# Two decoder layers on one core: the second mixer's end worked head by head, with the output rows in another order

## The chip, the cores and the metric

The kernel runs on one core of a Trainium2 chip. The metric is the device time of one execution, in microseconds. The kernel before took 1078.41 us, the median of three runs (1078.24 to 1080.96). One further execution was profiled; all rows below come from that one.

## The reference

The reference is one inference step through two decoder layers, for 256 prompt tokens and 64 sample tokens (8 sequences of 8), 320 columns in all, 1024 channels. Each layer is a mixer and a mixture of experts. The change lies in the second layer's mixer, whose core is:

```python
def odd_mixer(h, ...):
    gy, xb, q, k, v = split(h @ w_in)                 # 512 channels each
    xc = conv_b + sum(xe[:, i:i + L] * conv_w[i])     # causal, width 4
    r, ig = sigmoid(xc @ rgate_w + rgate_b), sigmoid(xc @ igate_w + igate_b)   # 8 blocks of 64
    log_a = -LRU_C * r * softplus(-lru_lambda);  a = exp(log_a)
    b = sqrt(-expm1(2 * log_a)) * ig * xc             # 1.0 in place of the root at position 0
    b[:, 0] += a[:, 0] * h0
    hs = scan over time of  h = a * h + b
    yc = gelu(gy) * hs
    o = dilated_attn(q, k, v)                         # 8 heads of 64, prompt and sample
    return concatenate([yc, o]) @ w_out
x = x + odd_mixer(rmsnorm(x));  x = x + hier_moe(rmsnorm(x))
```

The last state of the scan is an output too.

## The kernel before

Channels lie on the 128 partitions and tokens along the free axis. A tensor of 512 channels is thus four blocks of 128 x 320. The code calls each block j = 0 to 3; this document calls it a head of the recurrent part where the title does. The work of each engine is written out by hand in one fixed order, with semaphores that count what each engine has done. `MIX1_TENSOR`, `MIX1_SCALAR` and `MIX1_VECTOR` (L85 to L104) name those counts; `tensor_did`, `scalar_did` and `vector_did` wait for one of them. `next_reads` lets an instruction raise a count and makes DVE wait for it, so that its next instruction may read the result.

A weight matrix is used in two parts: `w_hi`, a rounded copy made by ACT, and `w_lo`, the rest, made by DVE. The same is done to the moving operand. A product is then three matmuls for each 128 channels (hi x hi, hi x lo, lo x hi). Weights come in chunks of 1 MB from a stream: SP loads chunk c into a `raw` buffer (`load_chunk`), ACT splits it (`split_hi`, L329), DVE makes the low part (`split_lo`, L341), and a `raw` buffer may be loaded again once `w_lo_made` says that its low part is done. A `w` buffer may be written again once TensorE's `tile_done` says that the rows of its last chunk are through.

The second mixer's output product is 8 rows of 128 channels, two per chunk (`AT_OUT1` to `AT_OUT1 + 3`); row i accumulates in PSUM bank i. `out1_rows` (L3061) makes row i over the channel blocks `ks`: blocks 4 to 7 are the attention's result, held in `attn_hi` and `attn_lo`, blocks 0 to 3 are the recurrent part's, held in `h_hi` and `h_lo`. There are only two `w` buffers in this stage, so the third chunk's split waits for rows 0 and 1, the fourth's for rows 2 and 3.

The stretch that changes is the mixer's end, behind the projection's tile 18:

- TensorE (`mix1_pe`, from L3036): the gates' products 4 to 7 (`gate`, L2871, banks 0 and 1 in turn) among the last attention work; projection tile 19, in bank 1; then, when tile 19 has been read and the attention's low parts are made (`y_lo` at 3), rows 0 to 3 over blocks 4 to 7; when the recurrent part's low parts are made (`y_lo` at 4), rows 0 to 3 over blocks 0 to 3; rows 4 to 7 whole, each followed by a piece of the router's work (`front_pe`).
- ACT (`mix1_act`, from L2535): the gates' tanh (`gate_out`), the square root `lru_root` over all four blocks (L2543), the attention's high parts (L2545 and L2547), half a weight chunk (L2549), gelu over all four blocks (L2551), the recurrent part's high part (L2553).
- DVE (`mix1_dve`, from L2819): `lru_square`; the copies of the last attention results; `lru_in` (L2706); the attention's low parts (L2831); tile 19 out of its bank (`tile_out(19)`); half a weight chunk's low part (L2835); `lru_scan` (L2717: four products with the root's result, called the weighing below; the samples' start values, L2724 to L2726; four scans; two copies of the last states); the product with gelu (L2838); the low part (L2841). Then `out_proj_dve` adds each finished row to `xt`.
- POOL stores the last states when `lru_kept` is counted (L3204). ACT waits for that store, in `moe_act` (L580), before it splits the first chunk of the experts' weights.

Of the kernel before, what the change touches and what calls it, by code (L numbers as in the profile page):

```python
# [16 lines left out]
ALU = mybir.AluOpType  # L17
# [10 lines left out]
HT = 4  # L28
# [49 lines left out]
def counted(*names):  # L78
# [13 lines left out]
                      "s_out2", "gate4", "s_turned30", "s_turned31", "s_turned32", "gate5", "p_turned7", "p_out6", "gate6", "s_values3", "gate7",  # L92
# [59 lines left out]
def decoder_layers(nc, ins, outs, stop=None):  # L152
    with ExitStack() as ctx:
# [2268 lines left out]
        def mix1_act(eng):  # L2422
# [120 lines left out]
            eng.activation(lru_m, lru_m, ACT.Sqrt, scale=0.25).then_inc(S("mix1_scalar"), 1)  # L2543
            vector_did(eng, "p_kept3")
# [4 lines left out]
            out_half(1).then_inc(S("w_hi_made"), 1)  # L2549
            eng.wait_ge(S("in1_taken"), IN1_TILES)  # L2550
            eng.activation(gy, gy, ACT.Gelu_apprx_tanh).then_inc(S("mix1_scalar"), 1)  # L2551
            vector_did(eng, "yc_made")
            eng.activation(h_hi[:, 0:4, :], gy, ACT.Copy).then_inc(S("y_hi"), 1)  # L2553

        def mix1_dve(eng):
# [161 lines left out]
            def lru_scan():  # L2717
                scalar_did(eng, "lru_root")
                next_reads(eng, eng.memset(lru_m[:, :, 0:1], 0.5))
                for j in range(HT):  # L2720
                    last = eng.tensor_tensor(lru_m[:, j, :], lru_m[:, j, :], lru_i[j], ALU.mult)
                next_reads(eng, last)
                starts = lambda v: v[:, :, TP:T].rearrange("p j (b s) -> p j b s", b=NB)[:, :, :, 0]
# [3 lines left out]
                for j in range(HT):  # L2727
                    last = eng.tensor_tensor_scan(lru_t[:, j, :], lru_a[:, j, :], lru_m[:, j, :], 0.0, ALU.mult, ALU.add)
                next_reads(eng, last)
# [93 lines left out]
            lru_square()  # L2823
            sample_masked(3)
            prompt_kept(3)
            sample_kept(3)
            lru_in()
            for n, cols in enumerate((slice(0, TP), slice(TP, T))):
                vector_did(eng, "attn_out3")
                eng.wait_ge(S("y_hi"), n + 2)  # L2830
                eng.tensor_tensor(attn_lo[:, :, cols], q1[:, :, cols], attn_hi[:, :, cols], ALU.subtract).then_inc(S("y_lo"), 1)  # L2831

            tile_out(19)
            eng.wait_ge(S("w_hi_made"), AT_OUT1 + 2)
            out_half_lo(1).then_inc(S("w_lo_made"), 1)  # L2835
            lru_scan()
            scalar_did(eng, "gelu")
# [15 lines left out]
        def mix1_pe(eng, begun):  # L2853
# [198 lines left out]
            for i in range(HT):  # L3052
                out1_rows(eng, i, (4, 5, 6, 7), True, False)
# [337 lines left out]
```

## Time and profile before

| | |
|---|---|
| median of three runs | 1078.41 us (1078.24 to 1080.96) |
| profiled execution | 1070.39 us, its span 1068.5 us |
| TensorE (PE) busy | 1033.6 us, 97% of the span |
| VectorE (DVE) busy | 815.6 us, 76% |
| ScalarE (ACT) busy | 639.8 us, 60% |
| mean granted TensorE clock | 0.989 |
| data moved | 271.04 MB, 254 GB/s over the span |

The span is the time from the first to the last instruction. A busy engine is not an engine at its peak. A matmul's duration includes its way through the array, so that neighbours overlap; what counts is the distance from start to start. The granted clock is given in parts of full speed. Where a line waits for several things, the profile names the one that came last.

### The profile page before, as it was taken

How to read it: one execution, taken by the hardware profiler on the slowest of the kernel's cores; microseconds unless marked ns; L12 is line 12 of the kernel's file. 1: busy time of each engine (PE TensorE's matmuls, PEld its weight loads, DVE VectorE, ACT ScalarE, POOL GpSimd, SP SyncE). 2: the span in 40 equal slices, each digit the busy share in tenths (PEclk: the TensorE clock that was granted, in tenths of full speed). 3: DMA queues.
4: the chain of work that ended last, by engine and by line, in shares of the span. 5: the costliest groups of instructions: out<-in, count | busy, mean ns of one | idle time of the engine just before them, and what ended most of it. 6: DMA issues, size and time to landing. Idle time of an engine off the chain costs nothing.

```text
span 1068.5 us, 17486 instructions
## 1 busy us (share of the span) xinstructions
PE 1033.6 (97%) x7349; PEld 871.5 (82%) x7349; DVE 815.6 (76%) x926; ACT 639.8 (60%) x660; POOL 19.0 (2%) x23
## 2 busy tenths in 40 slices
PE   9999999899999999999999999989999999999995
PEld 8899889877788888888878877677688888888884
DVE  7649545675788998999986677654878999998983
ACT  6556224524677767677755442445677777767664
POOL 0000000000000000000001300000000000000000
PEclk9999999999999999999999999989999999999998
DMA  9333000226399999999958779617199999999951
GB/s 373 132 115 107 21 4 3 73 80 248 133 343 347 368 362 360 362 362 369 354 221 349 296 281 376 257 41 275 53 353 324 375 351 355 357 365 366 372 212 52
DMA packets 40323, 271.04 MB, mean 254 GB/s; under 512 B 5057, under 2 KB 5521, under 8 KB 9521
## 3 DMA queue, kind: packets, MB, share of 16 engines
q1 hardware_dynamic: 39616, 267.11, 66.5%
q0 software_dynamic: 624, 2.76, 0.7%
q8 instruction: 61, 1.00, 0.4%
q14 instruction: 22, 0.17, 0.0%
HBM read 265.78 MB, written 4.07 MB: 253 GB/s over the span
## 4 chain that ended last, share of the span: by engine, by line
PE 84%; DVE 9%; ACT 3%; DMA 2%; issue 1%; ACTq 0%; SPq 0%; DVEq 0%
PE ps L925 11%; PE ps L927 11%; PE ps L926 11%; PE ps L959 5%; PE ps L961 5%; PE ps L960 5%; PE ps L352 3%; PE ps L354 3%; PE ps L353 3%; PE ps L1855 3%; DVE w_lo L346 2%; DMA raw<-in_stream 1%; PE ps L971 1%; PE ps L938 1%; PE ps L972 1%
## 5 line engine op out<-in xcount | busy, mean ns | idle before, releaser
L346 DVE TENSOR_TENSOR w_lo<-raw,w_hi 128x2048 fp32r<-128x2048 f32 x74 | 171.2, 2315 | 32.8 <-ACT w_hi L336 32.6
L336 ACT ACTIVATE w_hi<-raw 128x2048 fp32r<-128x2048 f32 x74 | 141.6, 1914 | 64.4 <-PE ps L927 25.8
L346 DVE TENSOR_TENSOR lo_more<-raw_more,hi_more 128x2048 fp32r<-128x2048 f32 x48 | 109.9, 2289 | 17.9 <-ACT hi_more L336 17.9
L346 DVE TENSOR_TENSOR lo_more<-raw,hi_more 128x2048 fp32r<-128x2048 f32 x48 | 109.9, 2290 | 11.9 <-ACT hi_more L336 11.9
L346 DVE TENSOR_TENSOR w_lo<-raw_more,w_hi 128x2048 fp32r<-128x2048 f32 x47 | 107.6, 2290 | 14.6 <-ACT w_hi L336 14.5
L336 ACT ACTIVATE hi_more<-raw 128x2048 fp32r<-128x2048 f32 x48 | 91.9, 1916 | 25.6 <-PE ps L927 25.6
L336 ACT ACTIVATE w_hi<-raw_more 128x2048 fp32r<-128x2048 f32 x47 | 90.1, 1917 | 16.2 <-PE ps L961 16.2
L336 ACT ACTIVATE hi_more<-raw_more 128x2048 fp32r<-128x2048 f32 x48 | 91.9, 1915 | 11.0 <-PE ps L961 9.6
L352 PE MATMUL ps<-h_hi,w_hi 128*128 128x320 f32 x272 | 87.1, 320 | 1.1 <-DVE arena L2579 1.1
L354 PE MATMUL ps<-h_hi,w_lo 128*128 128x320 f32 x272 | 84.6, 311 | 0.0
L353 PE MATMUL ps<-h_lo,w_hi 128*128 128x320 f32 x272 | 84.6, 311 | 0.0
L925 PE MATMUL ps<-hi_more,h_hi 128*128 128x512 f32 x170 | 68.1, 401 | 0.0
L926 PE MATMUL ps<-lo_more,h_hi 128*128 128x512 f32 x170 | 66.4, 391 | 0.0
L927 PE MATMUL ps<-hi_more,h_lo 128*128 128x512 f32 x170 | 66.3, 390 | 0.0
L925 PE MATMUL ps<-w_hi,h_hi 128*128 128x512 f32 x150 | 60.1, 401 | 0.0
L926 PE MATMUL ps<-w_lo,h_hi 128*128 128x512 f32 x150 | 58.5, 390 | 0.0
L927 PE MATMUL ps<-w_hi,h_lo 128*128 128x512 f32 x150 | 58.5, 390 | 0.0
L352 PEld LDWEIGHTS ps<-h_hi,w_hi 128*128 128x128 f32 x272 | 51.6, 190 | 5.0 <-issue 3.8
L959 PE MATMUL ps<-w_hi,hid_hi 128*128 128x512 f32 x136 | 53.5, 393 | 0.0
L961 PE MATMUL ps<-w_hi,hid_lo 128*128 128x512 f32 x136 | 53.0, 389 | 0.0
L960 PE MATMUL ps<-w_lo,hid_hi 128*128 128x512 f32 x136 | 52.9, 389 | 0.0
L353 PEld LDWEIGHTS ps<-h_lo,w_hi 128*128 128x128 f32 x272 | 51.8, 190 | 0.2
(538 smaller groups left out, 2401.8 us busy)
## 6 DMA issues: line engine op xcount, KB each, us to landing
raw<-in_stream SPq DMA_DIRECT2D x125, 1024.0 KB, 6.8
raw_more<-in_stream SPq DMA_DIRECT2D x96, 1024.0 KB, 6.9
arena<-in_k_near SPq DMA_DIRECT2D x6, 1024.0 KB, 10.4
arena<-in_v_near SPq DMA_DIRECT2D x5, 1024.0 KB, 7.6
arena<-in_k_far SPq DMA_DIRECT2D x6, 512.0 KB, 8.7
kv_spare<-in_v_near SPq DMA_DIRECT2D x3, 1024.0 KB, 8.8
arena<-in_v_far SPq DMA_DIRECT2D x5, 512.0 KB, 6.8
kv_spare<-in_k_near SPq DMA_DIRECT2D x2, 1024.0 KB, 13.5
```

The costliest lines, as they stand in the source:

```text
L336: eng.activation(hi_slot(W_SLOT[c]), raw_chunk(c), ACT.Copy).then_inc(S("w_hi_made"), 1)
L346: eng.tensor_tensor(lo_slot(W_SLOT[c]), raw_chunk(c), hi_slot(W_SLOT[c]), ALU.subtract).then_inc(S("w_lo_made"), 1)
L352: eng.matmul(ps[:, bank, 0:T], hi[:, m, k, :], x_hi[:, k, :], start=(k == 0), stop=False)
L353: eng.matmul(ps[:, bank, 0:T], hi[:, m, k, :], x_lo[:, k, :], start=False, stop=False)
L354: mm = eng.matmul(ps[:, bank, 0:T], lo[:, m, k, :], x_hi[:, k, :], start=False, stop=(k == KT - 1))
L925: eng.matmul(out, xh, hi[:, k, :], start=(n == 0 and k == 0), stop=False)
L926: eng.matmul(out, xh, lo[:, k, :], start=False, stop=False)
L927: mm = eng.matmul(out, xl, hi[:, k, :], start=False, stop=(n == 1 and k == 3))
L959: eng.matmul(out, hh[:, k, :], hi[:, k, :], start=(e % 4 == 0 and k == 0), stop=False)
L960: eng.matmul(out, hh[:, k, :], lo[:, k, :], start=False, stop=False)
L961: mm = eng.matmul(out, hl[:, k, :], hi[:, k, :], start=False, stop=(e % 4 == 3 and k == HT - 1))
L1855: mm = eng.matmul(at_head(bank, s, o), lhs[o:o + 64, s, :], rhs[o:o + 64, s, :], start=True, stop=True)
```

## The change

The last gate's product moves ahead of the last sample values on TensorE. ACT takes gelu of three blocks right behind the square root, ahead of the attention's high parts, and the fourth block's gelu and the recurrent part's high parts block by block behind them. `lru_starts` and `lru_kept` hold the instructions of the old scan's L2723 to L2726 and L2730 to L2731. On DVE the weighing is taken apart and moved ahead of the attention's low parts; tile 19 leaves its bank behind the first scan; scan, product with gelu and low part go block by block, and the half weight chunk and the last states come behind them. TensorE makes rows 0 and 2, then 1, over the attention's blocks; row 0 follows the recurrent blocks one by one; row 3's attention half comes behind row 1.

```diff
@@ tables @@
-                      "s_out2", "gate4", "s_turned30", "s_turned31", "s_turned32", "gate5", "p_turned7", "p_out6", "gate6", "s_values3", "gate7",
+                      "s_out2", "gate4", "s_turned30", "s_turned31", "s_turned32", "gate5", "p_turned7", "p_out6", "gate6", "gate7", "s_values3",
-                      "out_hi", "s_tok30", "s_tok31", "s_tok32", "p_tok7", "lru_root", "gelu")
+                      "out_hi", "s_tok30", "s_tok31", "s_tok32", "p_tok7", "lru_root", "gelu_most", "gelu")
-                      "s_masked3", "p_kept3", "attn_out3", "lru_kept", "yc_made")
+                      "s_masked3", "p_kept3", "attn_out3", "yc0", "yc1", "yc2", "yc3", "lru_kept")
@@ mix1_act @@
             eng.activation(lru_m, lru_m, ACT.Sqrt, scale=0.25).then_inc(S("mix1_scalar"), 1)
+            eng.wait_ge(S("in1_taken"), IN1_TILES - 1)
+            eng.activation(gy[:, 0:3, :], gy[:, 0:3, :], ACT.Gelu_apprx_tanh).then_inc(S("mix1_scalar"), 1)
             vector_did(eng, "p_kept3")
             eng.activation(attn_hi[:, :, 0:TP], q1[:, :, 0:TP], ACT.Copy).then_inc(S("y_hi"), 1)
             vector_did(eng, "attn_out3")
             eng.activation(attn_hi[:, :, TP:T], q1[:, :, TP:T], ACT.Copy).then_inc(S("y_hi"), 1)
-            out_half(1).then_inc(S("w_hi_made"), 1)
             eng.wait_ge(S("in1_taken"), IN1_TILES)
-            eng.activation(gy, gy, ACT.Gelu_apprx_tanh).then_inc(S("mix1_scalar"), 1)
-            vector_did(eng, "yc_made")
-            eng.activation(h_hi[:, 0:4, :], gy, ACT.Copy).then_inc(S("y_hi"), 1)
+            eng.activation(gy[:, 3, :], gy[:, 3, :], ACT.Gelu_apprx_tanh).then_inc(S("mix1_scalar"), 1)
+            for j in range(HT):
+                vector_did(eng, f"yc{j}")
+                eng.activation(h_hi[:, j, :], gy[:, j, :], ACT.Copy).then_inc(S("y_hi"), 1)
+                if j == 1:
+                    out_half(1).then_inc(S("w_hi_made"), 1)
@@ mix1_dve: lru_scan is taken apart into @@
+            def lru_weigh(js):
+                scalar_did(eng, "lru_root")
+                if js[0] == 0:
+                    next_reads(eng, eng.memset(lru_m[:, :, 0:1], 0.5))
+                for j in js:
+                    last = eng.tensor_tensor(lru_m[:, j, :], lru_m[:, j, :], lru_i[j], ALU.mult)
+                next_reads(eng, last)
+            def lru_starts():
...
+            def lru_scan(j):
+                next_reads(eng, eng.tensor_tensor_scan(lru_t[:, j, :], lru_a[:, j, :], lru_m[:, j, :], 0.0, ALU.mult, ALU.add))
+            def yc(j):
+                scalar_did(eng, "gelu" if j == 3 else "gelu_most")
+                eng.tensor_tensor(gy[:, j, :], gy[:, j, :], lru_t[:, j, :], ALU.mult).then_inc(S("mix1_vector"), 1)
+            def yc_lo(j):
+                vector_did(eng, f"yc{j}")
+                eng.wait_ge(S("y_hi"), j + 4)
+                eng.tensor_tensor(h_lo[:, j, :], gy[:, j, :], h_hi[:, j, :], ALU.subtract).then_inc(S("y_lo"), 1)
+            def lru_kept():
...
@@ mix1_dve, its end @@
             lru_square()
+            lru_in()
             sample_masked(3)
+            lru_weigh((0, 1))
             prompt_kept(3)
+            lru_weigh((2,))
             sample_kept(3)
-            lru_in()
+            lru_weigh((3,))
             for n, cols in enumerate((slice(0, TP), slice(TP, T))):
...
                 eng.tensor_tensor(attn_lo[:, :, cols], q1[:, :, cols], attn_hi[:, :, cols], ALU.subtract).then_inc(S("y_lo"), 1)
+            lru_starts()
+            lru_scan(0)
             tile_out(19)
+            yc(0)
+            lru_scan(1)
+            yc(1)
+            yc_lo(0)
+            lru_scan(2)
+            yc(2)
+            yc_lo(1)
+            lru_scan(3)
+            yc(3)
+            yc_lo(2)
+            yc_lo(3)
             eng.wait_ge(S("w_hi_made"), AT_OUT1 + 2)
             out_half_lo(1).then_inc(S("w_lo_made"), 1)
-            lru_scan()
-            scalar_did(eng, "gelu")
-            eng.tensor_tensor(gy, gy, lru_t, ALU.mult).then_inc(S("mix1_vector"), 1)
-            vector_did(eng, "yc_made")
-            eng.wait_ge(S("y_hi"), 4)
-            eng.tensor_tensor(h_lo[:, 0:4, :], gy, h_hi[:, 0:4, :], ALU.subtract).then_inc(S("y_lo"), 1)
+            lru_kept()
@@ mix1_pe @@
             gate(6)
+            gate(7)
             sample_values(3)
-            gate(7)
             prompt_values(7)
             sample_out(3)
             in1_tile(19)
+            eng.wait_ge(S("gate_taken"), 2 * HT)
+            eng.wait_ge(S("y_lo"), 3)
+            out1_rows(eng, 0, (4, 5, 6, 7), True, False)
+            out1_rows(eng, 2, (4, 5, 6, 7), True, False)
             eng.wait_ge(S("in1_taken"), IN1_TILES)
-            eng.wait_ge(S("y_lo"), 3)
+            out1_rows(eng, 1, (4, 5, 6, 7), True, False)
             for i in range(HT):
-                out1_rows(eng, i, (4, 5, 6, 7), True, False)
-            eng.wait_ge(S("y_lo"), 4)
-            for i in range(HT):
-                out1_rows(eng, i, (0, 1, 2, 3), False, True).then_inc(S("tile_done"), 1)
+                if i == 2:
+                    out1_rows(eng, 3, (4, 5, 6, 7), True, False)
+                out1_rows(eng, i, (0, 1, 2, 3), False, True, i == 0).then_inc(S("tile_done"), 1)
@@ out1_rows @@
+                if follow:
+                    eng.wait_ge(S("y_lo"), 4 + k)
```

## Rows read from the trace of the kernel before

**Rows 1.** The page, part 4: the chain that ended last, shares of the span

```profile
PE 84%; DVE 9%; ACT 3%; DMA 2%; issue 1%; ACTq 0%; SPq 0%; DVEq 0%
```

**Rows 2.** Windows: each engine's busy us (x instructions), TensorE clock, DMA share, GB/s

```profile
122.00:124.00 2.00, 0.50 (x20) 0.29 (x13) 1.93 (x4) 0.00 (x0) 0.00 (x0) 1.00 0.00 0
...
193.00:199.00 6.00, 6.00 (x64) 5.38 (x63) 4.25 (x4) 1.26 (x3) 0.00 (x0) 0.72 0.02 5
...
707.90:710.40 2.50, 0.03 (x1) 0.00 (x0) 1.45 (x2) 1.02 (x1) 0.54 (x1) 1.00 0.03 7
...
712.30:717.10 4.80, 4.80 (x18) 4.80 (x19) 0.49 (x1) 0.00 (x0) 0.00 (x0) 0.50 0.01 3
...
765.00:1050.00 285.00, 284.99 (x1330) 236.24 (x1329) 247.65 (x158) 203.53 (x144) 0.00 (x0) 1.00 0.87 326
```

**Rows 3.** TensorE's waits, 685 to 760 us: total us, times, longest

```profile
PE ps L3072 <- DVE h_lo L2841: 4.4, 1, 4.4
PE ps L971 <- DVE select_r L742: 1.1, 1, 1.1
PE ps L3072 <- DVE w_lo L346: 0.9, 1, 0.9
PE ps L3072 <- DVE arena L2579: 0.8, 1, 0.8
```

**Rows 4.** Timeline of TensorE: start us, us, line, output and inputs, x count

```profile
689.66 0.81 PE L2874 MATMUL ps<-arena 128*128 128x320 f32 x2
...
705.13 0.31 PE L3072 MATMUL ps<-attn_hi,w_hi 128*128 128x320 f32 x1
...
706.01 0.31 PE L3072 MATMUL ps<-attn_hi,w_hi 128*128 128x320 f32 x1
```

**Rows 5.** The chain in order of time, 670 to 780 us: start us, us, what

```profile
699.87 1.07 ACT w_hi L2477
...
712.30 0.63 PE ps L3072
...
718.40 1.92 ACT w_hi L336
...
722.70 0.41 PE ps L3072
```

**Rows 6.** Timeline of ACT; in brackets its idle time before, and what ended it

```profile
694.95 1.28 ACT L2543 ACT_TABLE_LOAD   x1
...
700.94 1.28 ACT L2551 ACT_TABLE_LOAD   x1
702.24 1.28 ACT L2551 ACTIVATE arena<-arena 128x1280 f32<-128x1280 f32 x1
```

**Rows 7.** Timeline of DVE, 690 to 713 us

```profile
690.68 1.49 DVE L2715 SCALAR_TENSOR_TENSOR arena<-arena 128x1280 f32<-128x1280 f32 x1
...
696.34 1.29 DVE L2709 SCALAR_TENSOR_TENSOR attn_low<-attn_low,arena 128x320 f32<-128x320 f32 x3
...
698.59 1.56 DVE L2831 TENSOR_TENSOR attn_lo<-arena,attn_hi 128x1024 fp32r<-128x1024 f32 x2 [0.57 <-ACT attn_hi L2545]
700.07 0.48 DVE L2579 TENSOR_TENSOR arena<-ps,arena 128x320 f32<-128x320 f32 x1
...
702.24 1.30 DVE L2721 TENSOR_TENSOR arena<-arena,attn_low 128x320 f32<-128x320 f32 x3
...
703.98 0.22 DVE L2724 TENSOR_TENSOR arena<-arena 128x32 f32<-128x32 f32 x1
...
704.68 2.97 DVE L2728 TENSOR_TENSOR_SCAN arena<-arena 128x320 f32<-128x320 f32 x4
...
710.75 1.49 DVE L2841 TENSOR_TENSOR h_lo<-arena,h_hi 128x1280 fp32r<-128x1280 f32 x1 [1.40 <-ACT h_hi L2553]
```

**Rows 8.** DMA issues, 700 to 765 us: queue, count, KB each, median us to landing

```profile
raw<-in_stream SPq DMA_DIRECT2D x5, 1024.0 KB, 4.9
...
out_lru<-state POOLq DMA_DIRECT2D x1, 18.0 KB, 1.7
```

More of the change, by code:

```diff
@@ L2715, in lru_square @@
                 eng.scalar_tensor_tensor(flat(lru_m), flat(lru_t), 1.0, flat(lru_m), ALU.add, ALU.mult).then_inc(S("mix1_vector"), 1)
-            def lru_scan():
+            def lru_weigh(js):
                 scalar_did(eng, "lru_root")
-                next_reads(eng, eng.memset(lru_m[:, :, 0:1], 0.5))
-                for j in range(HT):
+                if js[0] == 0:
+                    next_reads(eng, eng.memset(lru_m[:, :, 0:1], 0.5))
+                for j in js:
                     last = eng.tensor_tensor(lru_m[:, j, :], lru_m[:, j, :], lru_i[j], ALU.mult)
                 next_reads(eng, last)
+            def lru_starts():
                 starts = lambda v: v[:, :, TP:T].rearrange("p j (b s) -> p j b s", b=NB)[:, :, :, 0]
@@ L2726, in lru_scan @@
                 next_reads(eng, eng.memset(starts(lru_a), 0.0))
-                for j in range(HT):
-                    last = eng.tensor_tensor_scan(lru_t[:, j, :], lru_a[:, j, :], lru_m[:, j, :], 0.0, ALU.mult, ALU.add)
-                next_reads(eng, last)
+            def lru_scan(j):
[8 more added lines that the diff above has]
+            def lru_kept():
                 eng.tensor_copy(lru_out[:, :, 0:1], lru_t[:, :, TP - 1:TP])
@@ L3059, in mix1_pe, with out1_rows @@
                 front_pe(eng, 1, i)
-        def out1_rows(eng, i, ks, start, stop):
+        def out1_rows(eng, i, ks, start, stop, follow=False):
             c = AT_OUT1 + i // 2
```

## The prediction

> **What bounds the kernel now.** I read the chain first: 84% of it is TensorE [rows 1]. So a microsecond counts only where TensorE waits or runs slowly. The windows say where that is not: from 765 to 1050 us TensorE is busy 284.99 of 285 us at full clock [rows 2], so the expert stage cannot shrink, only start earlier. TensorE's own waits between 685 and 760 us say where it is: the longest, 4.4 us, is for `h_lo` of L2841, and another 0.9 us is for the weights' low part [rows 3]. Behind the 4.4 us comes a second cost. In 707.90 to 710.40 TensorE is all but idle at full clock; the 18 matmuls of 712.30 to 717.10 run at a granted 0.50, which is 1.2 GHz [rows 2]. They take 4.80 / 18 = 0.267 us each. At 1.00, 2.4 GHz, six of the same matmuls take 0.88 us (705.13 to 706.01), 0.147 each [rows 4]. The slow stretch costs 18 x 0.120 = 2.2 us.
>
> The end of the stretch is the chain: output rows 0 and 1 need all of `h_lo` (712.30), then ACT splits the third weight chunk (718.40), DVE makes its low part, and row 4 starts at 722.70 [rows 5]. I take the start of row 4 as the mark; everything behind it hangs on it.
>
> **Part 1, the last gate's product first.** A gate's product lasts 0.81 us, about 0.73 from start to start [rows 4]. gate(7) moves ahead of the sample values of pair 3, which move back by as much; TensorE's sum stays. It now follows gate(6), which began at 689.66, and ends near 691.2, so its tanh leaves ACT near 691.8. ACT's square root waited for that tanh alone: its table load started at 694.95, right behind it [rows 6], while the other input, `lru_square`, was done at 690.68 + 1.49 = 692.17 [rows 7]. So root: 692.2 + 1.28 + 1.28 = 694.8. The sample output waits for a masked product that comes 0.7 us later; the last prompt values, which TensorE runs in between at their old time, cover it. Cost 0 (0 to +0.2).
>
> **Part 2, gelu of three heads ahead of the attention's split.** It adds one table load of 1.28 and 960 columns. 1280 columns took 1.28 [rows 6], so about 1.0. ACT: 694.8 + 2.3 = 697.1, when the attention split may begin; its first 1024 columns take 1.05 (estimate, from 1280 in 1.28). That is sooner than `attn_lo` had them, at 698.59 [rows 7], so nothing is lost. On DVE `lru_in` (three in 1.29 [rows 7] and a fourth of 0.48, to about 694.0), the masked product, three weighings and the two copies lie ahead of it, and end near 697.7. The four weighings (1.29 + 0.48 = 1.8, from 702.24 on [rows 7]) come off the tail. DVE then waits for ACT's first `attn_hi` near 698.15, and `attn_lo`, 1.56 for two [rows 7], ends near 699.7. Tile 19's last result is there before 699.87, when ACT, waiting for it, starts [rows 5]. TensorE thus begins rows 0 and 2 at 699.75; before, it began 0.8 us later, waiting for DVE to empty tile 19's bank (L2579) [rows 3]. That wait goes, since these two rows use other banks.
>
> The row on the table load shows the switch whole: ACT's work of 699.87 ran 1.07 us [rows 5], the load began at 700.94, gelu at 702.24 [rows 6]. The Trainium skill, "ScalarE: Activation LUTs", section "What ACT_TABLE_LOAD costs", gives a load of about 1283 ns and a drain of about 1380 ns on top. The load agrees with the trace, the drain does not show. By that rule the two switches ahead of the attention split would cost 2.8 us more and the time would be about 1073.8; this case's row 700.94 speaks against it. What such a mechanism would do here, in this trace's own numbers, is rival B.
>
> **Part 3, DVE's tail by heads.** Pitches from the rows [rows 7]: a 320-column product lasts 0.48, and three in 1.29 give a pitch of 0.41. Four scans took 2.97 without a wait between; one scan with its round trip is 0.83 (estimate: 0.80 and 0.03). The sample starts take 704.68 - 703.98 = 0.70. From `attn_lo`'s end at 699.7:
> starts 0.70, scan 0 0.83, tile 19 out 0.41, yc0 0.41: 702.05. Scan 1 0.83, yc1 0.41, low 0 0.41: 703.7. Scan 2, yc2, low 1, again 1.65: 705.35. Scan 3 0.83, yc3 0.41, low 2 0.41: 707.0. Low 3 waits for ACT's copy of head 3 (yc3 ends at 706.66; the copy, a quarter of 1280 columns plus start, about 0.46), begins at 707.2 and ends at 707.7.
> Before, `h_lo` ended at 710.75 + 1.49 = 712.24 [rows 7]. The 4.5 us are: weighings 1.8, the second half of the weight split with the wait ahead of it 1.6 (now last), the ACT hand-over of 1.4 (now beside the next head), less the finer grain. Tile 19 leaves its bank 1.2 us later, at 701.7. Row 1 wants it at 703.3, behind 24 matmuls of rows 0 and 2, so that wait is covered; without the new order it would show. ACT's copies fit: head 0 at 702.3 behind the last gelu, head 1 at 703.4, then half a weight chunk of 1.07 [rows 5] to 704.9, head 2 at 705.05 (low 2 wants it at 706.6).
>
> **Part 4, output rows in another order.** 36 matmuls at 0.147 are 5.3 us: 699.75 to 705.05. Then row 0 follows the heads: k0 to 705.5 (its low part is there at 703.8), k1 to 706.0, k2 waits until 707.1, k3 until 707.75. Idle 1.1 + 0.2 us against 4.4. Row 0 is issued by 708.2, row 1 by 710.0. Its last matmul lasts 0.31 [rows 4]: ACT begins the third chunk at 710.2, and the old 4.3 us (718.40 to 722.70 [rows 5]) give 714.5. TensorE meanwhile has row 3's attention half and both last halves, 36 matmuls, to 715.25. The weights are no longer late; row 4 starts at 715.25. The low part of the second half chunk (1024 columns, about 1.2 against 1.49 for 1280 [rows 7], now 707.65 to 708.9) is wanted at 710.0.
>
> **What is moved later.** That low part frees a buffer for the first expert chunk: SP issues its load at 708.9 instead of near 702.2, where the old low part ended (the weighings follow it at 702.24 [rows 7]), and it lands after a median 4.9 us [rows 8], near 714. ACT wants it near 719, behind the fourth chunk and a table load. The LRU rows are stored from about 709.7, a little over 1 us later than before, with 1.7 us to landing [rows 8], against ACT's wait for them near 719. Both cost 0, with 5 us to spare.
>
> **The sum.** 722.70 - 715.25 = 7.45 us. The same from the terms: `h_lo` 4.5 earlier; behind it 15 matmuls of 2.2 in place of 24 with the slow clock, 5.9: 3.7; together 8.2; less 0.8 of the old wait for weights that is now work: 7.4. Behind row 4 all waits keep their distances (ACT's token squares come 1 us closer, but their readers had 2 us and more), and the expert stage is TensorE without a gap. I take 7.4 us. The profiled execution took 1070.39 us (span 1068.5), 8.0 under the median of 1078.41. The stretch is fixed work, so I subtract the same: **1078.4 - 7.4 = 1071.0 us**. Bounds of the doubtful terms: the scan's round trip between 0.74 (a quarter of 2.97) and 0.9 moves the sum by +0.3 to -0.3; starts and copies by 0.3; the clock below.
>
> **Rivals.**
> A. The clock falls all the same. TensorE still has 1.3 us of idle near 706 to 707.8. For a fall: in 193 to 199 us the clock stood at a mean of 0.72 although TensorE was busy throughout [rows 2], so a dense row of matmuls does not exclude it. Against: in 122 to 124 us TensorE was busy only 0.50 of 2 us and stayed at 1.00, and in 707.90 to 710.40 it held through 2.5 us [rows 2]; here dense work surrounds a shorter gap. Price as before, 2.2 us: 1073.2. Chance 0.10.
> B. A table switch with work queued behind it costs a second time its 1.28 us [rows 6], because ACT empties first. There are two ahead of the attention split, 2.6 us. The split, `attn_lo` and DVE's tail are all 2.6 later, TensorE starts at 702.3, and row 4 at 717.85. Gain 4.85: 1073.6. Against it is the gapless row 700.94. Chance 0.03.
> C. No visible change: the gain returns as a later wait behind row 4, for instance DVE's additions and the tokens' low parts, ahead of which the same FIFO now has the LRU rows. It needs more than 4.2 us of new waiting, while TensorE's only longer wait there besides those counted is one of 1.1 us [rows 3]. About 1077. Chance 0.08.
> D. Slower: the first expert chunk's load, issued 6.7 us later. ACT stands at its split with all token work behind it. Tokens' squares and copies take 5 us behind the load, the low parts 1.9, and TensorE wants them near 731. So a landing up to 724 is free; from 724 + 7.4 = 731.4 on, 22.5 us after issue, the kernel is slower, one for one. For it: ACT is strictly in order. Against: median 4.9 us [rows 8] and an almost empty queue. At 25 us: 1081. Chance 0.04.
> The forecast has 0.75, its own range 1070.2 to 1072.2. Runs of before spread over 2.7 us, so 0.3% (3.2 us) is what can be told from no change. Range 1069.5 to 1075.8: below, the bounds' 0.6 and 0.9 for the runs' spread; above, A and B together (1071.0 + 2.2 + 2.6). Faster 0.87 (forecast, A, B, less a margin), same 0.08, slower 0.05.
>
> **What would show it.** Right: TensorE's wait for `h_lo` about 1.3 us in place of 4.4; granted clock 1.00 from 700 to 725; row 4 starting 15.5 us after the first attention matmul of the output (before 22.1) with no wait for weights; one gelu load near 694.8; `tile 19` out about 1.6 us behind `attn_lo`. Wrong: a clock of 0.50 behind 707; a gap between the square root and gelu; TensorE waiting for tile 19's bank ahead of row 1; ACT waiting on the first expert chunk's DMA; or a saving at row 4 that is gone at 765.

## The result and the profile after

The changed kernel took a median of 1066.92 us in 12 runs. The kernel before took 1075.14 us in 12 runs (1069.88 to 1080.96), among them the three that the forecast started from. One run of the changed kernel (1280.74 us at a mean granted clock of 0.747) and one of `rows_paired` below (1709.39 us at 0.552) were disturbed: without them the two medians are 1066.61 us (1062.63 to 1072.61) and 1064.70 us, and every ratio leaves them out. The ratio is 0.9936, with a 95% interval of 0.9914 to 0.9958: 6.9 us faster, and the interval excludes no change. A second series (`after_again`, below) gave 1067.51 against 1072.84, ratio 0.9939 (0.9913 to 0.9964), or 6.5 us. The medians by themselves lie 8.2 and 5.3 us apart in the two series; I go by the ratios. The forecast was 1071.0 us with a range of 1069.5 to 1075.8, or a ratio of 1071.0 / 1078.41 = 0.9931. So size and mechanism came out, and the absolute time fell below the range. Both halves of that need showing.

The two profiled executions mislead by their totals: 1070.39 us before (span 1068.5), 1070.92 us after (span 1069.1). I therefore measure from a place that both have: the start of DVE's second `lru_square` pass. It is at 690.68 us before [rows 7] and at 699.16 after. Nothing that leads up to it was changed; only gate(7), moved forward on TensorE, begins some 0.3 us ahead of it. In the table every time is counted from that place, which I call the mark. "Row 4" is the start of output row 4, "router" the start of DVE's first instruction of the router, L719 (`router_filled`'s expectation calls it the weighing, which is not the recurrent part's weighing), and "end" the span's end, known to 0.1 us.

```
                        before                  after
first row, attention    9.93                    8.73
row 4                  32.02                   24.12
router (L719)          57.30                   49.32
end                   377.82                  369.94
```

The changed kernel gains 7.90 us at row 4 and still 7.88 at the end, while its execution was 0.5 us longer. The missing 8.5 us (699.16 - 690.68) lie ahead of the mark, in code that is the same; `before_second` below shows that they come from the first mixer. The kernel before was profiled twice more there, with row 4 at 32.43 and 32.30, so the gain at row 4 is 7.9 to 8.3 us. TensorE's waits in the changed kernel, 685 to 760 us (in total, times, longest), against [rows 3]:

```profile
PE ps L971 <- DVE select_r L742: 1.1, 1, 1.1
PE ps L3106 <- DVE h_lo L2745: 0.8, 1, 0.8
PE ps L524 <- DVE hot L730: 0.4, 1, 0.4
```

The wait of 4.4 us for `h_lo` is now 0.8; those for tile 19's bank (0.8) and for the weights' low part (0.9) are gone. Here are its windows from the mark to the first row, to the start of row 0's last block, to row 4, and over the stretch that the prediction named, in the columns of [rows 2]:

```profile
699.16:707.89 8.73, 8.73 (x96) 6.86 (x95) 7.92 (x18) 6.99 (x8) 0.00 (x0) 1.00 0.07 26
707.89:715.70 7.81, 7.02 (x47) 6.51 (x46) 7.33 (x16) 3.24 (x6) 0.00 (x0) 1.00 0.00 0
715.70:723.28 7.58, 7.58 (x52) 7.58 (x52) 4.82 (x7) 1.92 (x1) 0.55 (x1) 1.00 0.40 143
...
700.00:725.00 25.00, 24.21 (x198) 22.25 (x189) 19.71 (x40) 12.77 (x15) 0.55 (x1) 1.00 0.18 58
```

The granted clock is 1.00 throughout, where the 18 matmuls behind the old gap ran at 0.50 [rows 2]. TensorE's rows of the timeline: the first attention product, the only listed wait, row 4.

```profile
707.89 0.31 PE L3106 MATMUL ps<-attn_hi,w_hi 128*128 128x320 f32 x1
...
715.00 0.41 PE L3106 MATMUL ps<-h_hi,w_hi 128*128 128x320 f32 x1 [0.79 <-DVE h_lo L2745]
...
723.28 0.31 PE L3106 MATMUL ps<-h_hi,w_hi 128*128 128x320 f32 x1
```

From the first to the last are 15.39 us (before 22.09; forecast 15.5). ACT, against [rows 6], shows the one thing better than forecast:

```profile
699.53 0.53 ACT L2439 ACTIVATE arena<-ps,half_bias 128x320 f32<-128x320 f32 x1
700.08 1.28 ACT L2543 ACT_TABLE_LOAD   x1
701.37 1.27 ACT L2543 ACTIVATE arena<-arena 128x1280 f32<-128x1280 f32 x1
702.66 1.28 ACT L2545 ACT_TABLE_LOAD   x1
703.96 1.00 ACT L2545 ACTIVATE arena<-arena 128x960 f32<-128x960 f32 x1
704.87 1.04 ACT L2547 ACTIVATE attn_hi<-arena 128x1024 fp32r<-128x1024 f32 x1
```

The square root's table load starts at 700.08, right behind the last tanh, while its input `lru_square` ends only at 700.65 (the first row of DVE's fence below: 699.16 + 1.49). The forecast had put the load behind that input. The first profile of the kernel before already had loads that ran ahead of a late input, and also one that did not:

```profile
593.94 1.28 ACT L2483 ACT_TABLE_LOAD   x1
599.09 0.20 ACT L2483 ACTIVATE state<-state 128x4 f32<-128x4 f32 x1 [3.86 <-DVE state L2598]
...
608.86 1.28 ACT L2461 ACT_TABLE_LOAD   x1 [5.88 <-DVE state L2641]
```

What decides between the two no run here shows. DVE of the changed kernel, against [rows 7]:

```profile
699.16 1.49 DVE L2719 SCALAR_TENSOR_TENSOR arena<-arena 128x1280 f32<-128x1280 f32 x1
...
706.04 1.56 DVE L2852 TENSOR_TENSOR attn_lo<-arena,attn_hi 128x1024 fp32r<-128x1024 f32 x2 [0.29 <-ACT attn_hi L2547]
...
708.22 0.82 DVE L2736 TENSOR_TENSOR_SCAN arena<-arena 128x320 f32<-128x320 f32 x1
709.07 0.49 DVE L2583 TENSOR_TENSOR arena<-ps,arena 128x320 f32<-128x320 f32 x1
709.48 0.48 DVE L2740 TENSOR_TENSOR arena<-arena 128x320 f32<-128x320 f32 x1
...
715.15 0.49 DVE L2745 TENSOR_TENSOR h_lo<-arena,h_hi 128x320 fp32r<-128x320 f32 x1 [0.20 <-ACT h_hi L2555]
```

The last low part ends at 715.64, 16.48 from the mark; before, 21.56. Of that 5.08, 4.54 is what part 3 of the prediction had. The other 0.54 fits the earlier table load (0.57): ACT goes from it to `attn_hi` without a gap, and DVE waits 0.29 us for `attn_hi` in the row of 706.04. No run moved the load alone.

### The profile page after: what moved, and what is told of

It is laid out like the page before. It is cut to its first block, busy times and chain, and to the rows that moved or that the text cites. A ratio compares the mean times of both kernels' runs of the same rounds, so it can differ in the third digit from the quotient of the medians.

```text
span 1069.1 us, 17507 instructions
## 1 busy us (share of the span) xinstructions
PE 1038.7 (97%) x7349; PEld 876.2 (82%) x7349; DVE 816.1 (76%) x932; ACT 640.6 (60%) x664; POOL 18.8 (2%) x23
## 4 chain that ended last, share of the span: by engine, by line
PE 85%; DVE 8%; ACT 3%; DMA 2%; issue 1%; SPq 1%; ACTq 0%; DVEq 0%
PE ps L925 11%; PE ps L927 11%; PE ps L926 11%; PE ps L959 5%; PE ps L961 5%; PE ps L960 5%; PE ps L352 3%; PE ps L353 3%; PE ps L354 3%; PE ps L1855 3%; DMA raw<-in_stream 2%; PE ps L971 1%; PE ps L938 1%; DVE w_lo L346 1%; PE ps L972 1%
```

## Experiments

Four questions: what is each part worth, how much of it is clock, where does the run-to-run level come from, and where do the timed 6.5 to 6.9 us lose a little against 7.9. The four undoings come first; each is the changed kernel with one part taken back, seen in one profile. The number that counts is row 4's start, 24.12 in the changed kernel.

**gate_back.**

```diff
@@ mix1_pe, and the same in MIX1_TENSOR @@
             gate(6)
-            gate(7)
             sample_values(3)
+            gate(7)
```

> The changed kernel with one part undone: gate(7) again behind the sample values of pair 3. The measure is the distance from the start of DVE's second lru_square pass (which lies ahead of everything that was changed) to TensorE's start of output row 4: 32.0 us in the kernel before, 24.1 in the changed one. Theory: everything on ACT and DVE hangs on the last gate's tanh now, because lru_in stands ahead of the sample's masked product. The tanh ends near 703.4 on the changed kernel's scale instead of 700.06, so root, gelu and the attention's split come 3.3 us later and the distance is 27.2 +- 0.4. Rival: as my forecast had it, the gate's place is a matter of order on TensorE whose cost is covered; then 24.1 to 24.4.

Measured: 27.45 from the mark, 3.3 us later than in the changed kernel; 1069.8 us. TensorE's longest waits, and DVE's rows that they hang on:

```profile
PE ps L2993 <- DVE arena L2652: 2.3, 1, 2.3
PE ps L3106 <- DVE h_lo L2745: 0.9, 1, 0.9
```

```profile
697.60 1.30 DVE L2713 SCALAR_TENSOR_TENSOR attn_low<-attn_low,arena 128x320 f32<-128x320 f32 x3 [2.79 <-ACT arena L2439]
...
699.53 0.48 DVE L2652 SCALAR_TENSOR_TENSOR arena<-ps,state,consts 128x256 f32<-128x256 f32 x1
```

DVE's queue now has `lru_in` ahead of the sample's masked product; with the gate late, `lru_in` waits 2.79 us for its tanh, the masked product behind it is late, and TensorE's sample output waits 2.3 us for that. So the gate's place is worth 3.3 us here, because it lets `lru_in` and the recurrent part's weighing stand so early. What it would gain alone, in the kernel before, was not run.

**gelu_behind.**

```diff
             eng.activation(lru_m, lru_m, ACT.Sqrt, scale=0.25).then_inc(S("mix1_scalar"), 1)
-            eng.wait_ge(S("in1_taken"), IN1_TILES - 1)
-            eng.activation(gy[:, 0:3, :], gy[:, 0:3, :], ACT.Gelu_apprx_tanh).then_inc(S("mix1_scalar"), 1)
...
             eng.activation(attn_hi[:, :, TP:T], q1[:, :, TP:T], ACT.Copy).then_inc(S("y_hi"), 1)
+            eng.activation(gy[:, 0:3, :], gy[:, 0:3, :], ACT.Gelu_apprx_tanh).then_inc(S("mix1_scalar"), 1)
```

> The changed kernel with the gelu of the first three blocks put behind the attention's high parts. Distance as above (24.1 in the changed kernel). Theory: ACT stands idle for 3.4 us behind the attention's high parts, which holds the table load of 1.28 and the 1.0 of gelu, and ahead of them it waits for DVE's copy of the attention's result anyway; so 24.1, between 24.0 and 24.3. Rival: the early gelu is what lets the heads follow each other, and behind it the first product with gelu waits for the table: 25.1 to 26.4.

Measured: 24.00, 0.1 us earlier than with gelu ahead; 1068.17 us. ACT in this kernel:

```profile
700.85 1.06 ACT L2545 ACTIVATE attn_hi<-arena 128x1024 fp32r<-128x1024 f32 x1 [2.09 <-DVE arena L2680]
701.82 0.40 ACT L2547 ACTIVATE attn_hi<-arena 128x256 fp32r<-128x256 f32 x1
702.23 1.28 ACT L2549 ACT_TABLE_LOAD   x1
703.53 1.01 ACT L2549 ACTIVATE arena<-arena 128x960 f32<-128x960 f32 x1
```

Gelu moved behind the split ends at 704.54 and still has over 1 us of idle behind it; ahead of the split it fills the 2.1 us that ACT here waits for DVE. Both places are free, so gelu's place ahead of the split is worth nothing. This does not price part 2 as a whole: the old place, all four blocks behind tile 19's reading, was not run. By this kernel's rows it would be late: ACT begins the fourth block at 709.60 in the changed kernel, and a load of 1.28 and 1280 columns in 1.28 [rows 6] from there end near 712.2, where the first product with gelu now begins at 709.48 (an estimate).

**rows_old.** TensorE makes the output rows in the old order.

```diff
-            eng.wait_ge(S("gate_taken"), 2 * HT)
-            eng.wait_ge(S("y_lo"), 3)
-            out1_rows(eng, 0, (4, 5, 6, 7), True, False)
-            out1_rows(eng, 2, (4, 5, 6, 7), True, False)
             eng.wait_ge(S("in1_taken"), IN1_TILES)
-            out1_rows(eng, 1, (4, 5, 6, 7), True, False)
+            eng.wait_ge(S("y_lo"), 3)
+            for i in range(HT):
+                out1_rows(eng, i, (4, 5, 6, 7), True, False)
+            eng.wait_ge(S("y_lo"), 7)
             for i in range(HT):
-                if i == 2:
-                    out1_rows(eng, 3, (4, 5, 6, 7), True, False)
-                out1_rows(eng, i, (0, 1, 2, 3), False, True, i == 0).then_inc(S("tile_done"), 1)
+                out1_rows(eng, i, (0, 1, 2, 3), False, True).then_inc(S("tile_done"), 1)
```

> The changed kernel with TensorE's old order: rows 0 to 3 over the attention's blocks behind tile 19's reading, then a wait for all four recurrent low parts, then rows 0 to 3. Theory: the start waits for tile 19's bank (709.6 instead of 707.9), 48 matmuls end at 716.7, behind the last low part, rows 0 and 1 end near 720.2 and the third chunk's two splits of 4.35 us are late again by 1.2 us: 25.7 +- 0.3. Rival: only the 1.1 us of idle within row 0 moves elsewhere and the order is worth nothing: 24.1 +- 0.3.

Measured: 27.59, 3.5 us later; 1075.93 us. TensorE's waits from the mark to the router's start:

```profile
PE ps L3103 <- DVE w_lo L2771: 1.7, 1, 1.7
PE ps L3103 <- DVE arena L2583: 1.6, 1, 1.6
PE ps L3103 <- DVE w_lo L346: 0.9, 1, 0.9
```

The wait for tile 19's bank (L2583) is the one the prediction said the new order covers. That for the half chunk's low part (L2771) I had not counted in the expectation, which was 1.9 us too low: in the changed DVE order that low part comes last, and the old row order wants it for row 3's attention half, ahead of all recurrent blocks. Row order and DVE order only work together.

**heads_off.** The new orders stay, but scan, gelu product, `h_hi` and `h_lo` are each done over four blocks again, as before.

```diff
@@ mix1_act @@
-            for j in range(HT):
-                vector_did(eng, f"yc{j}")
-                eng.activation(h_hi[:, j, :], gy[:, j, :], ACT.Copy).then_inc(S("y_hi"), 1)
-                if j == 1:
-                    out_half(1).then_inc(S("w_hi_made"), 1)
+            out_half(1).then_inc(S("w_hi_made"), 1)
+            vector_did(eng, "yc3")
+            eng.activation(h_hi[:, 0:4, :], gy, ACT.Copy).then_inc(S("y_hi"), 4)
@@ mix1_dve: four scans, tile_out(19) behind the first, then @@
+            eng.tensor_tensor(gy, gy, lru_t, ALU.mult).then_inc(S("mix1_vector"), 4)
+            vector_did(eng, "yc3")
+            eng.wait_ge(S("y_hi"), 7)
+            eng.tensor_tensor(h_lo[:, 0:4, :], gy, h_hi[:, 0:4, :], ALU.subtract).then_inc(S("y_lo"), 4)
```

> The changed kernel with scans, product with gelu, high and low part in whole passes again (the weighing stays ahead, the last weights stay behind, the rows keep their new order). Theory: the last low part comes only 0.35 us later (716.0), but row 0 can't begin before it; rows 0 and 1 end 1.7 us later and row 4 starts at 24.85 + 0.8 = 25.7 +- 0.3. TensorE then idles near 2.9 us ahead of row 0; the clock may fall, which adds up to 2.2 (27.9). Rival: the split by heads is the main part of the gain (my forecast named the hand-over of 1.4 and the overlap): 27 or more with the clock at full.

Measured: 25.99, 1.9 us later; 1071.23 us, with one wait:

```profile
PE ps L3100 <- DVE h_lo L2861: 3.0, 1, 3.0
```

TensorE stood still for 3.0 us and the clock stayed at 1.00 behind it; in the kernel before it fell behind 4.4. The blocks are worth 1.9 us (the whole passes on ACT and DVE together), about half of what one might read out of 4.4 against 0.8.

The undoings sum to 3.3 - 0.1 + 3.5 + 1.9 = 8.6 us against a gain of 7.9: the parts lean on each other. Each rests on one profile. Now the other side, the kernel before with one thing added.

**gap_filled.** 28 matmuls that do nothing fill the wait for `h_lo`.

```diff
@@ the kernel before, mix1_pe, ahead of the recurrent half of the rows @@
+            for _ in range(28):
+                eng.matmul(ps[:, 5, 0:T], attn_hi[:, 0, 0:P], attn_hi[:, 0, :], start=True, stop=True)
             eng.wait_ge(S("y_lo"), 4)
```

> The kernel before with 28 dummy matmuls of 320 columns (their result is never read) put into TensorE's idle time ahead of the wait for the recurrent low parts. Distance from DVE's second lru_square pass to row 4: 32.0 in the kernel before. Theory: the clock of 0.50 behind the gap is owed to the gap; filled, it stays at 1.00, rows 0 and 1 take 3.5 instead of 5.7 us, and the distance is 29.8 +- 0.2. Rival: the fall comes from something else, or the dummies push row 0 back: 32.0 or more.

Measured: row 4 at 29.81 from the mark, against 32.02: 2.2 us, which is the prediction's 18 x 0.120. Against the two later profiles of the kernel before (32.43 and 32.30) it is 2.6 and 2.5. The wait for `h_lo` is down to 0.3. Its clock where the 18 matmuls run now:

```profile
722.00:724.00 2.00, 2.00 (x16) 2.00 (x15) 0.49 (x1) 0.00 (x0) 0.00 (x0) 1.00 0.00 0
```

The execution as a whole took 1078.41 us, above the 1072.90 of the kernel before timed beside it. The mark lies at 699.55 us here, against 690.68 in the first profile: it is again the stretch ahead of the mark that is long.

**weigh_alone.** The kernel before with the recurrent part's weighing right behind `lru_in`.

```diff
             lru_in()
+            lru_weigh()
@@ and lru_scan() without these four products @@
```

> The kernel before with one part done alone: the four weighing products ahead of the attention's low parts. Theory: 1.8 us leave the tail, but 1.3 of them push the attention's low parts, tile 19's reading and the weight half back, since ACT's high parts are there first, less 0.4 us of a wait that goes: the last low part comes 0.9 us earlier and the distance is 31.1 +- 0.3 if the clock still falls, 28.9 if it does not. Rival: the whole 1.8 us are gained, 30.2.

Measured: 28.72, 3.3 us earlier than before, though the clock did fall. TensorE's waits for DVE, and windows around the fall:

```profile
PE ps L3075 <- DVE arena L2579: 2.2, 1, 2.2
...
PE ps L3075 <- DVE h_lo L2844: 0.5, 1, 0.5
```

```profile
706.00:707.00 1.00, 0.63 (x4) 0.64 (x5) 1.00 (x2) 0.99 (x2) 0.00 (x0) 1.00 0.00 0
707.00:711.00 4.00, 4.00 (x19) 4.00 (x18) 3.83 (x8) 0.94 (x1) 0.00 (x0) 0.57 0.66 209
711.00:713.00 2.00, 2.00 (x16) 2.00 (x15) 1.68 (x4) 0.26 (x1) 0.54 (x1) 1.00 0.30 116
...
717.00:724.00 7.00, 6.13 (x42) 5.87 (x41) 3.49 (x4) 2.85 (x2) 0.00 (x0) 1.00 0.00 0
```

I had expected 31.1 with a fall and 28.9 without. The fall moved: it now follows the earlier wait of 2.2 us and slows the attention half of the rows, which had idle time behind it to lose (the wait for `h_lo` is 0.5 in place of 4.4). The slow clock thus cost nothing at row 4, and 2.2 us of clock and 1.06 of an earlier `h_lo` (20.50 against 21.56 from the mark) make the 3.3. So the weighing alone is worth only 1.06 on DVE's tail, not 1.8. That the fall moved because of the longer first wait (2.2 in place of 0.8) is read from one profile and not tested.

**after_again** and **rows_paired**, timed together. The first is the changed kernel once more. In the second, output rows 0 and 1 alternate between the blocks as these come, which gives TensorE work for its last wait.

```diff
-            for i in range(HT):
-                if i == 2:
-                    out1_rows(eng, 3, (4, 5, 6, 7), True, False)
-                out1_rows(eng, i, (0, 1, 2, 3), False, True, i == 0).then_inc(S("tile_done"), 1)
+            for k in range(HT):
+                eng.wait_ge(S("y_lo"), 4 + k)
+                for i in range(2):
+                    mm = out1_rows(eng, i, (k,), False, k == HT - 1)
+                    if k == HT - 1:
+                        mm.then_inc(S("tile_done"), 1)
+            out1_rows(eng, 3, (4, 5, 6, 7), True, False)
+            for i in range(2, HT):
+                out1_rows(eng, i, (0, 1, 2, 3), False, True).then_inc(S("tile_done"), 1)
```

> The changed kernel once more, beside the kernel before on the same chip. Theory: the absolute time of a run is set by how long the clock stands at half in the first mixer, which the change does not touch, so the medians of both kernels move together by several us between sessions while their difference stays: ratio 0.992 to 0.995 (6 to 8 us). The distance to row 4 is 24.1. Rival: the profiled pair, 1068.5 before and 1069.1 after, shows that the gain is lost elsewhere: ratio 0.998 to 1.000.

> The changed kernel with rows 0 and 1 following the recurrent blocks together (block 0 for both rows, block 1 for both, and so on). Theory: six matmuls instead of three stand ahead of each wait, which covers the 0.8 and 0.3 us that TensorE still idles; row 4 starts 1.1 us earlier, distance 23.0 +- 0.2, time 1.1 us below the changed kernel (0.1%, at the edge of what the timing shows). Rival: the third chunk's split, which waits for both rows, or the low part of the second half chunk becomes the bound and the distance stays at 24.1.

Measured: `after_again` 24.11 from the mark, so in the changed kernel the stretch repeats to 0.01 us. `rows_paired` 23.05, with no wait of TensorE left between the mark and the router's start. Timed, the ratio is 0.994 (0.991 to 0.9969) against 0.9939: the 1.1 us are in the profile and can't be told in the runs, which spread over 8 us. (The median of all 8 runs is 1067.08 us, of 7 of them 1064.70.)

**thin_mixed.** `rows_paired` with 12 wide matmuls that do nothing among the thin ones of the first mixer, where the clock falls near 67 us.

```diff
+            def wide():
+                for _ in range(2):
+                    eng.matmul(ps[:, 6, 0:T], h_hi[:, 0, 0:P], h_hi[:, 0, :], start=True, stop=True)
@@ behind each of the sums over a head, L1650 and L1697 @@
+                    wide()
```

> As rows_paired, and in the first mixer 12 dummy matmuls of 320 columns (never read) are mixed into the 48 matmuls of one or two columns ahead of which the clock fell near 66 to 69 us in both profiles. Theory: that fall is owed to a stretch of thin matmuls, not to idle time; the dummies cost 1.8 us and save the fall there, 2 to 5 us: the profile has no clock below 1.00 between 60 and 80 us and the time is 0 to 3 us below rows_paired. Rival: the fall comes anyway or moves, and the time is 1.8 us above rows_paired.

Measured: the clock falls all the same, for 11 us; 1069.66 us (12 runs, ratio 0.995, 0.9926 to 0.9973). The theory failed; the rival, the cost of the added work on top of `rows_paired`, is what remains.

```profile
66.00:67.00 1.00, 1.00 (x11) 1.00 (x10) 0.36 (x3) 1.00 (x1) 0.00 (x0) 1.00 0.00 0
67.00:78.00 11.00, 11.00 (x50) 11.00 (x49) 2.54 (x3) 0.31 (x1) 0.00 (x0) 0.53 0.29 95
```

TensorE was busy in every microsecond around it. Thin matmuls at that place are not the cause, or 12 wide ones are not enough; which, I did not try.

**before_second** and **before_third**, the kernel before profiled twice more.

> The kernel before, unchanged, profiled a second time, to see whether what the change removed is there in every execution. If it is: from the start of the second lru_square pass, output row 4 begins 32.0 us later, with a stretch of half clock of nearly 7 us behind the wait for the gelu product's low part, as in the first profile, and the change is worth 7.9 us in every execution. If the clock falls there only in some executions: 29.8 us, and the change is worth 5.7 us in these, which would put the timed 6.5 to 6.9 us between the two. The span itself is to differ from the first profile's 1068.5 us by up to 10 us, by half clock in the first mixer.

> As the second profile of the kernel before: 32.0 us from the second lru_square pass to output row 4 if the clock falls in the gap each time, 29.8 us where it does not.

Measured: row 4 at 32.43 and 32.30 from the mark (32.02 in the first profile), each time behind a wait of 4.4 us and with the clock down. The second took 1080.88 us, the third 1071.33. Windows of 60 to 80 and 193 to 213 us, first of the kernel before in the first profile, then of its second one, then of the changed kernel's profile:

```profile
60.00:80.00 20.00, 20.00 (x153) 19.34 (x153) 7.31 (x17) 12.28 (x23) 0.00 (x0) 0.91 0.30 106
193.00:213.00 20.00, 18.50 (x172) 16.51 (x170) 11.89 (x10) 10.58 (x14) 0.00 (x0) 0.89 0.24 77
```

```profile
60.00:80.00 20.00, 20.00 (x117) 20.00 (x117) 6.82 (x13) 10.34 (x20) 0.00 (x0) 0.74 0.30 105
193.00:213.00 20.00, 18.02 (x186) 15.66 (x183) 8.99 (x10) 12.61 (x15) 0.54 (x1) 0.57 0.18 60
```

```profile
60.00:80.00 20.00, 20.00 (x117) 20.00 (x117) 6.42 (x14) 9.63 (x19) 0.00 (x0) 0.74 0.31 105
193.00:213.00 20.00, 18.02 (x163) 15.39 (x158) 8.99 (x10) 12.95 (x15) 0.54 (x1) 0.57 0.17 60
```

The last two agree, and the first does not: the same code gets a mean clock of 0.57 or 0.89 in 193 to 213 us, whichever kernel it belongs to. Over all 16 profiles the mark lies at 690.7 us where the two windows have the highest clocks (`before`: 0.91 and 0.89; `rows_paired`: 0.91 and 0.91), and near 699 us or later wherever they are at 0.74 to 0.83 and 0.57 to 0.60, except for 697.43 in `router_filled_second`. Why the clock is low for longer in one execution than in another no run shows. The mark lies at 690.68, 700.80 and 699.16 us in these three; 10.1 of the 10.5 us between the two profiles of before (1080.88 - 1070.39) are there. The timed runs fit: over 21 runs of the changed kernel, time falls by 0.88 us for each 0.001 of mean granted clock (0.981 to 0.992), and leaves 0.47 us unexplained (least squares over these runs).

**router_filled**, profiled twice. By then one difference was open. From the router's start (L719) to the end takes 320.5 us in all three profiles of before (320.52, 320.57, 320.48) and in the first of the changed kernel (320.62), but 322.17 in `after_again` and 322.26 in `rows_paired`. In `after_again`, the windows from the end of TensorE's wait for `select_r` (1.1 us, the line as in the changed kernel's first profile):

```profile
752.00:753.00 1.00, 0.30 (x3) 0.04 (x1) 0.97 (x7) 0.00 (x0) 0.00 (x0) 1.00 0.03 8
753.00:757.00 4.00, 3.61 (x9) 2.89 (x10) 3.65 (x18) 3.41 (x3) 0.00 (x0) 0.58 0.00 0
757.00:762.00 5.00, 5.00 (x21) 3.31 (x20) 2.83 (x9) 2.44 (x4) 0.00 (x0) 1.00 0.01 3
```

Behind the wait of 1.1 us for the router's places, which the kernel before has as well [rows 3], the clock falls to 0.50 for the first gather products: 1.6 us. It is there in seven of the nine profiles taken so far without the fall in the output rows (six of eight of changed kernels, which the expectation below miscounts by one each, and `gap_filled`), and in none of the four with it. The edit adds 6 of the matmuls that already fill TensorE's time there:

```diff
             mm.then_inc(S("placed"), 1)
-            filler(6)
+            filler(12 if layer else 6)
```

> The changed kernel with 6 more of the matmuls that do nothing ahead of TensorE's wait for the second router's places (12 in place of 6; 0.133 us each at full clock by the spacing of the ones there, 0.8 us of the 1.09 us of idle time). In three profiles of the kernel before, in which the clock falls in the gap of the output rows, it never falls at this wait; in five of seven profiles of changed kernels without that fall it falls here, 9 matmuls take 0.43 us in place of 0.23 from one to the next, and the end comes 1.6 us later. Theory one, the clock falls because of this idle time: with 0.3 us of it left, no half clock from the wait on for 10 us, start of the weighing to end 320.5 us in every profile, and a median 1 us below the changed kernel's at equal falls elsewhere. Theory two, the fall is due at about this place whatever TensorE does: 322.1 us as before. If the added ones run past the wait's end, the first gather product comes later and the distance is longer than 320.5 by as much.

> The same kernel profiled again: without a fall at the router a second time if the idle time is the cause; with one in about two profiles of three if it is not.

Measured: 320.58 us from the router's start to the end in both, and 24.11 and 24.10 at row 4. The wait shrank to 0.2 us and the clock held:

```profile
745.85 2.02 PE L513 MATMUL ps<-h_hi 128*128 128x320 f32 x12
748.09 0.47 PE L971 MATMUL ps<-select_r,tok_hi 128*128 128x512 f32 x1 [0.21 <-issue]
748.39 0.39 PE L972 MATMUL ps<-select_r,tok_lo 128*128 128x512 f32 x1
```

Timed: 1064.54 us (8 runs, 1061.44 to 1066.64), ratio to before 0.9907 (0.9874 to 0.994). That interval overlaps the changed kernel's 0.9914 to 0.9958, so the 1.6 us are shown by the profiles and not by the timing.

**paired_filled** has both edits.

> Both edits on the changed kernel: output rows 0 and 1 alternate between the heads as these come, and 6 more matmuls that do nothing at the router. Row 4 begins 23.05 us after the second lru_square pass (24.1 in the changed kernel), and there is no fall at the router: about 1.1 us below router_filled, and 1.1 to 2.7 us below the changed kernel. If the router's fall is not tied to its idle time, 1.1 us below the changed kernel.

Measured: row 4 at 23.05, router to end 320.55, so 368.79 from the mark to the end, the shortest together with `thin_mixed` (368.80), which happened to have no fall at the router. Timed 1064.89 us (9 runs, ratio 0.9919, 0.9885 to 0.9953), not told apart from `router_filled`. The fall at the router is absent from three profiles of three with the filler, and from two of eight of changed kernels without it. That speaks for the idle time as the cause; at the rate of those eight, luck would give three of three with a chance of about 0.02 (0.25 cubed).

## Why the prediction was right or wrong

**The level, wrong.** The step that failed is the last one: "The stretch is fixed work, so I subtract the same" from 1078.41, with 0.9 us in the range "for the runs' spread". The subtraction was right, the base was not. 1078.41 was a median of three runs of a kernel whose runs go from 1069.9 to 1081.3 us; its median over 12 runs was 1075.14, over 23 others, timed later, 1072.84. With these the same 7.4 us give 1067.7 and 1065.4, and 1066.92 was measured. Luck had a part: of the 32 other runs only 5 are as high as the lowest of those three. But the profile showed the warning. Its execution took 8.0 us less than the median, the prediction noted it, and then wrote "Runs of before spread over 2.7 us" without it; with it the spread was 10.6. What moves the level is the clock granted in the first mixer (0.57 or 0.89 over 20 us), which no step of the prediction looked at beyond 193 to 199 us [rows 2].

**The sum, right, 0.5 us small.** Forecast 7.45 us at row 4, measured 7.90. DVE's last low part came 0.54 us sooner than forecast (16.48 from the mark, against 707.7 - 690.68 = 17.02), which fits the 0.57 that the table load gained: the forecast's "692.2 + 1.28 + 1.28" put the load behind `lru_square`, and only the square root itself waits for that. The rows of 593.94 in the same profile could have told it. Timed, 6.5 to 6.9 us arrive: in six of the eight profiles of changed kernels without the filler the fall of the clock at the router takes 1.6 us back. That is rival C's kind, a later loss, at about a quarter of C's 6 us and by another mechanism; I had no row that pointed to it, since the kernel before never shows it.

**Part 1, right with a gap.** "Cost 0" holds. But the 3.3 us that `gate_back` loses show that the forecast gave this part no price where it carries the early weighing.

**Part 2, half right.** Gelu ahead of the split costs nothing (0.1 us in `gelu_behind`), and brings nothing against a place right behind it. Both loads took 1.28 us with no gap behind the square root (701.37 + 1.27 = 702.64, load at 702.66), which is rival B's refutation. The Trainium skill, "ScalarE: Activation LUTs", section "What ACT_TABLE_LOAD costs", has a drain of about 1380 ns on top: neither switch shows it.

**Part 3, right.** From the scan's start to that of tile 19's reading 0.85 (forecast 0.83), from there to the gelu product 0.41, blocks at a pitch of 1.66 (708.22 to 709.88; forecast 1.65). "`tile 19` out about 1.6 us behind `attn_lo`": its reading starts 1.47 behind. TensorE's idle was 0.79 and 0.15, forecast 1.1 and 0.2.

**Part 4, right.** No wait for weights, none for the bank. `rows_old` puts the row order at 3.5 us, more than the 0.8 for the bank and 0.9 for the weights, because the DVE order behind it depends on it too.

**Rivals.** A did not happen in either profile of the changed kernel between the mark and the router; its price of 2.2 us fits `gap_filled` (2.2 to 2.6). D did not: ACT's waits from 716 to 748 us are all for TensorE, none for a transfer.

## What to carry to other kernels

Compare profiles from an instruction that both kernels have to one behind the change, not by their totals: here totals said +0.5 us and the stretch said -7.9, and it repeated to 0.02 us over four profiles in the changed order and to 0.4 over three of the kernel before. Before taking a median of three runs as the level, see how far the profiled execution is from it, count that execution into the spread, and look for stretches of half clock in code that the change leaves alone; a gap of several us there belongs in the range. And when a fall of the clock is removed at one wait, look at the next short wait ahead of dense work, and price putting work into it.

## What the hardware showed that was not expected

- ACT's table load need not wait for its activation's input: it began at 700.08 us with the input ready at 700.65, and at 593.94 in the kernel before, 5.15 us ahead of its activation. It does not always run ahead: the load of 608.86 came only behind a wait of 5.88 us.
- The clock can fall behind a short wait or not, in the same code: behind 1.1 us at the router in six of eight profiles of changed kernels, while it held behind 3.0 us in `heads_off` and fell behind 4.4 and 2.2 us in the kernel before and `weigh_alone`.
- In the first mixer it fell to 0.50 with TensorE busy in every microsecond (67 to 78 us in `thin_mixed`). There and in 193 to 213 us the length of the fall differed from one execution to the next; together the two moved the mark by 10.1 us between two profiles of the same kernel.
- A fall can cost nothing: in `weigh_alone` a slow stretch of 4 us (mean clock 0.57) lay over matmuls with idle time behind them.
